# Running totals of a state space mixer made once for four token tiles, and broadcast by turning a column of step zero

## The reference, cut to what matters

```
a_cs = jnp.cumsum(ac, axis=-1)                       # within a tile of 128 tokens
seg = a_cs[..., :, None] - a_cs[..., None, :]
decay = jnp.exp(jnp.where(causal, seg, -jnp.inf))
...
decay_to_end = jnp.exp(a_cs[..., -1:] - a_cs)
chunk_decay = jnp.exp(a_cs[..., -1])
y_off = jnp.einsum('bclgn,bcgkpn,bcgkl->bclgkp', cm, prev, jnp.exp(a_cs))
```

## Time and profile before

| | |
|---|---|
| median of 3 runs | 2507.09 us (2497.56 to 2507.71) |
| time of the profiled execution | 2508.93 us |
| its span | 2506.9 us |
| mean granted TensorE clock | 0.966 |
| instructions | 29324 |
| DMA, mean over the span | 89 GB/s |

### The profile page before, as it was taken

One profiled execution on the slowest core, in us unless ns is written; L12 is line 12 of the kernel. 1 busy time (PEld: TensorE's weight loads), 2 busy tenths in 40 slices (PEclk: granted clock), 3 DMA queues, 4 the chain that ended last, 5 costly groups with the idle time before them and its releaser, 6 DMA issues.

```text
span 2506.9 us, 29324 instructions
## 1 busy us (share of the span) xinstructions
PE 2345.6 (94%) x11988; PEld 1945.1 (78%) x11988; DVE 1307.2 (52%) x1935; ACT 922.7 (37%) x1670; POOL 155.0 (6%) x115
## 2 busy tenths in 40 slices
PE   7997888898999999999898999999899899899988
PEld 6887676776888888888686788888697687788766
DVE  4997677654834334635463573334525526413444
ACT  3353563433423223344333333233334425323343
POOL 0000100040400000400021040000000000000000
PEclk9998989899999999999899999999899999999999
DMA  5322223432332323312332223333232121221102
GB/s 156 99 86 68 85 89 135 132 116 84 94 123 96 101 94 99 119 51 68 112 99 67 71 100 102 100 101 101 67 118 81 37 90 62 68 84 51 34 34 109
DMA packets 187195, 224.78 MB, mean 90 GB/s; under 512 B 16603, under 2 KB 153510, under 8 KB 186038
## 3 DMA queue, kind: packets, MB, share of 16 engines
q1 hardware_dynamic: 174800, 191.90, 24.3%
q10 hardware_dynamic: 11686, 22.62, 2.6%
q0 software_dynamic: 576, 8.39, 0.9%
HBM read 213.72 MB, written 9.18 MB: 89 GB/s over the span
## 4 chain that ended last, share of the span: by engine, by line
PE 82%; DVE 11%; ACT 5%; issue 2%; ACTq 1%; POOL 0%; DVEq 0%
PE gemm L588 24%; PE gemm L589 23%; PE gemm L590 23%; PE aux L720 2%; DVE y_plain L2284 2%; DVE w_lo L2078 2%; PE aux L972 1%; PE aux L953 1%; PE aux L1225 1%; DVE x_lo L2101 1%; DVE work L2216 1%; PE aux L1247 1%; ACT w_hi L1291 1%; PE aux L1238 1%; DVE w_lo L2074 1%
## 5 line engine op out<-in xcount | busy, mean ns | idle before, releaser
L588 PE MATMUL gemm<-x_hi,w_hi 128*128 128x512 f32 x1288 | 518.2, 402 | 10.3 <-DVE w_lo L2078 7.9
L2078 DVE TENSOR_TENSOR w_lo<-raw,w_hi 128x1024 fp32r<-128x1024 f32 x250 | 317.8, 1301 | 392.0 <-ACT w_hi L1291 391.3
L590 PE MATMUL gemm<-x_hi,w_lo 128*128 128x512 f32 x1288 | 505.9, 393 | 0.0
L589 PE MATMUL gemm<-x_lo,w_hi 128*128 128x512 f32 x1288 | 505.7, 393 | 0.0
L1291 ACT ACTIVATE w_hi<-raw 128x1024 fp32r<-128x1024 f32 x250 | 254.0, 1051 | 246.7 <-PE gemm L590 243.6
L588 PE MATMUL gemm<-w_hi,x_hi 128*128 128x256 f32 (+2 forms) x992 | 315.5, 318 | 10.3 <-DVE h L2165 5.4
L588 PEld LDWEIGHTS gemm<-x_hi,w_hi 128*128 128x128 f32 x1288 | 244.1, 190 | 87.8 <-issue 24.0
L589 PE MATMUL gemm<-w_lo,x_hi 128*128 128x256 f32 (+2 forms) x992 | 310.6, 313 | 0.0
L590 PE MATMUL gemm<-w_hi,x_lo 128*128 128x256 f32 (+2 forms) x992 | 310.2, 313 | 0.0
L590 PEld LDWEIGHTS gemm<-x_hi,w_lo 128*128 128x128 f32 x1288 | 244.0, 189 | 52.1
L589 PEld LDWEIGHTS gemm<-x_lo,w_hi 128*128 128x128 f32 x1288 | 244.5, 190 | 46.9
(11 more groups left out here) (328 smaller groups left out, 2880.7 us busy)
## 6 DMA issues: line engine op xcount, KB each, us to landing
raw<-in_mlp_w_dram SPq DMA_DIRECT2D x64, 1024.0 KB, 5.2
raw<-in_w_in_dram SPq DMA_DIRECT2D x31, 1024.0 KB, 5.3
raw<-in_odd_w_in_dram SPq DMA_DIRECT2D x12, 1024.0 KB, 5.3
raw<-in_even_w_in_dram SPq DMA_DIRECT2D x10, 1024.0 KB, 5.3
raw<-in_even_w_in_dram SPq DMA_DIRECT2D x16, 512.0 KB, 5.3
raw<-in_xa_w_k_dram SPq DMA_DIRECT2D x8, 1024.0 KB, 5.0
raw<-in_xa_w_v_dram SPq DMA_DIRECT2D x8, 1024.0 KB, 5.0
raw<-in_even_w_out_dram SPq DMA_DIRECT2D x8, 1024.0 KB, 5.2
```

Source lines behind the costliest of these rows:

```text
L588: pe.matmul(dst, a_hi, b_hi, start=first, stop=False)
L589: pe.matmul(dst, a_hi, b_lo, start=False, stop=False)
L590: return pe.matmul(dst, a_lo, b_hi, start=False, stop=last)
L2078: dve.tensor_tensor(w_lo[:, s % W_SLOTS, :, :], raw[:, s // 2 % RAW_SLOTS, :, half], w_hi[:, s % W_SLOTS, :, :].bitcast(F32), ALU.subtract)\
```

## The change

- The state space sums of all four tiles are made by one `running_sums()`, with a second product with all ones for the tiles' totals. VectorE's `tile_sums()` copies the sums over the steps in `sm[:, 0:4]`, the totals to `sm[:, 8:12]`, total less sum to `sm[:, 12:16]`, and releases ScalarE once, after that. It stands in pass n = 0; VectorE's `differences` and the later tile sums are gone.
- ScalarE's `sum_exps()` exponentiates these once, after the first `decays`; the two small Exps of each tile are gone.
- The rows of sums are no products any more. The sums are already in a column, and a transpose of the column read with step zero puts them in a row on all partitions: one `turn` a head in `sums_as_rows`, four a head in `key_sums`. Before the first of either, TensorE waits until VectorE has written the sums (`aux_read(pe, "acs")`, `aux_read(pe, "cc")`).

```diff
--- before.py
+++ after.py
@@ -140,12 +140,12 @@
     def tile(c):
         return [("bc", c, q) for q in range(4)] + [("cb", c), ("xs", c, 0), ("xs", c, 1), ("bt", c)]
 
-    e += [("acs", 0)] + tile(0)
+    e += [("acs",)] + tile(0)
     for c in range(TT):
         for g in range(2):
             e += [("yd", c, g)] + ([("yo", c, g)] if c else [])
         if c + 1 < TT:
-            e += [("st", c, g) for g in range(2)] + [("acs", c + 1)] + tile(c + 1)
+            e += [("st", c, g) for g in range(2)] + tile(c + 1)
         e += [("yt", c, g) for g in range(2)]
     e += [("ln", "conv", i) for i in range(2)]
 
@@ -281,7 +281,7 @@
         cst = sb("cst", [P, 4])
         mxs = sb("mxs", [P, 3, 4])
         rs = sb("rs", [P, 3, 4])
-        sm = sb("sm", [P, 16, SH])
+        sm = sb("sm", [P, 20, SH])
         stats = sb("stats", [P, TT, 2, 6])
         mean_var = sb("mean_var", [P, TT, 2])
         rstd = sb("rstd", [P, 2, TT])
@@ -812,10 +812,13 @@
             for t in range(TT):
                 ins = turn(dst[:, SH * t:SH * (t + 1)], DTR[:, t * P:(t + 1) * P])
             ins.then_inc(aux_done, 1)
-            def running_sums(c):
+            def running_sums():
 
                 pe.wait_ge(S["dta_ready"], 1)
-                pe.matmul(next_aux("acs", c)[:, 0:SH], triu[:, :], sm[:, c, :], start=True, stop=True)\
+                dst = next_aux("acs")
+                steps = sm[:, 0:TT, :].rearrange("p a b -> p (a b)")
+                pe.matmul(dst[:, 0:TT * SH], triu[:, :], steps, start=True, stop=True)
+                pe.matmul(dst[:, TT * SH:2 * TT * SH], ones[:, :], steps, start=True, stop=True)\
                   .then_inc(aux_done, 1)
 
             def sums_as_rows(c):
@@ -824,8 +827,7 @@
                     dst = next_aux("bc", c, q)
                     for j in range(4):
                         hd = 4 * q + j
-                        ins = pe.matmul(dst[:, j * P:(j + 1) * P], sm[:, c, hd:hd + 1].broadcast_to([P, P]),
-                                        triu[:, :], start=True, stop=True)
+                        ins = turn(dst[:, j * P:(j + 1) * P], sm[:, c, hd:hd + 1].broadcast_to([P, P]))
                     ins.then_inc(aux_done, 1)
 
             def memory_steps(count):
@@ -885,9 +887,10 @@
             turned_memory()
             gemm("conv_in", x_hi, x_lo, panels=2)
             gemm("xbc", x_hi, x_lo, panels=4)
-            running_sums(0)
+            running_sums()
             gemm("xbc", x_hi, x_lo, panels=2)
             gemm("z", x_hi, x_lo, panels=3)
+            aux_read(pe, "acs")
             tile_operands(0)
             gemm("z", x_hi, x_lo, panels=1)
             aux_read(pe, "mem", 3)
@@ -915,7 +918,6 @@
                     for g in range(2):
                         pe.matmul(next_aux("st", c, g)[:, :], BT[:, g, :], XW[:, 8 * g:8 * g + 8, :],
                                   start=True, stop=True).then_inc(aux_done, 1)
-                    running_sums(c + 1)
                     memory_steps(1)
                     tile_operands(c + 1)
                 else:
@@ -1243,15 +1245,14 @@
 
                 dst = next_aux("cb_c", hd)
                 for t in range(TT):
-                    for s in range(t + 1):
-                        ins = pe.matmul(dst[:, t * P:(t + 1) * P], sm[:, s, hd:hd + 1].broadcast_to([P, P]),
-                                        (triu if s == t else ones)[:, :], start=(s == 0), stop=(s == t))
+                    ins = turn(dst[:, t * P:(t + 1) * P], sm[:, 4 + t, hd:hd + 1].broadcast_to([P, P]))
                 ins.then_inc(aux_done, 1)
 
             def next_key_sums(u):
                 if u[1] == 1 and u[0] + 1 < 8:
                     key_sums(u[0] + 1)
 
+            aux_read(pe, "cc")
             key_sums(0)
             units("c", [(hd, t) for hd in range(8) for t in range(TT)], scores_c, turns_c, values_c, next_key_sums)
             turned_output("Ct", "c", 2)
@@ -1585,23 +1586,25 @@
 
             def differences(c):
 
-                r = 8 + 4 * (c % 2)
+                act.wait_ge(S["seg_ready"], 1)
                 for q in range(4):
-                    act.wait_ge(S["seg_ready"], 4 * c + q + 1)
                     bank = wait_aux(act, ("bc", c, q))
                     for j in range(4):
                         hd = 4 * q + j
                         ins = act.activation(M[:, hd, :], bank[:, j * P:(j + 1) * P], ACT.Relu, scale=-1.0,
-                                             bias=sm[:, r, hd:hd + 1])
+                                             bias=sm[:, c, hd:hd + 1])
                     free_aux(ins, ("bc", c, q))
 
             def decays(c):
 
-                r = 8 + 4 * (c % 2)
                 aux_read(act, "bc", c, 3)
                 act.activation(M, M, ACT.Exp, scale=-1.0).then_inc(S["decay_ready"], 1)
-                step(act.activation(sm[:, r + 1:r + 3, :], sm[:, r + 1:r + 3, :], ACT.Exp))
-                act.activation(sm[:, r + 3, :], sm[:, r, :], ACT.Exp).then_inc(S["dte_ready"], 1)
+
+            def sum_exps():
+
+                act.wait_ge(S["seg_ready"], 1)
+                act.activation(sm[:, 8:16, :], sm[:, 8:16, :], ACT.Exp)
+                step(act.activation(sm[:, 16:20, :], sm[:, 0:4, :], ACT.Exp))
 
             def tile_rows(c):
 
@@ -1636,10 +1639,10 @@
             gate_z(3)
             logs()
             decays(0)
+            sum_exps()
             conv_first(KC - 1)
             split_to(FIRST_PANEL["xk0"] + 1)
             for c in range(TT):
-                r = 8 + 4 * (c % 2)
                 if c:
                     if c == 3:
                         act.wait_ge(S["k_out"], 16)
@@ -1647,7 +1650,7 @@
                 if c + 1 < TT:
                     act.wait_ge(S["xdt_ready"], c + 1)
                     for hd in range(SH):
-                        ins = act.activation(XW[:, hd, :], XDT[:, hd, :], ACT.Copy, scale=sm[:, r + 1, hd:hd + 1])
+                        ins = act.activation(XW[:, hd, :], XDT[:, hd, :], ACT.Copy, scale=sm[:, 12 + c, hd:hd + 1])
                     ins.then_inc(S["xw_ready"], 1)
                 if c:
                     memory_rows(c - 1, 1)
@@ -2342,34 +2345,27 @@
                     dve.scalar_tensor_tensor(sm[:, 0:4, :], dt, -1.0, over(row16[:, 1, :], TT), ALU.mult, ALU.mult)\
                        .then_inc(S["dta_ready"], 1)
 
-            def tile_sums(c):
-
-                r = 8 + 4 * (c % 2)
-                bank = wait_aux(dve, ("acs", c))
-                free_aux(dve.tensor_copy(sm[:, r, :], bank[:, 0:SH]), ("acs", c))
-                aux_read(dve, "acs", c)
+            def tile_sums():
+
+                bank = wait_aux(dve, ("acs",))
+                rows = bank[:, 0:2 * TT * SH].rearrange("p (i t n) -> p i t n", i=2, n=SH)
+                step(dve.tensor_copy(sm[:, 0:4, :], rows[:, 0]))
+                dve.tensor_copy(sm[:, 8:12, :], rows[:, 1])
+                free_aux(dve.tensor_tensor(sm[:, 12:16, :], rows[:, 1], sm[:, 0:4, :], ALU.subtract), ("acs",))
+                aux_read(dve, "acs")
+                dve.engine_nop().then_inc(S["seg_ready"], 1)
 
             for n in range(4):
                 split_to(FIRST_PANEL["z"] + n + 1)
                 taps(6)
                 if n == 0:
-                    tile_sums(0)
+                    tile_sums()
                 if n == 1:
                     accumulate(0)
                 if n == 2:
                     accumulate(1)
             tri2 = over(triu[:, :], 2)
             cb = TMP[:, 0, 0:2 * P].rearrange("p (a b) -> p a b", b=P)
-
-            def differences(c):
-
-                r = 8 + 4 * (c % 2)
-                for q in range(4):
-                    bank = wait_aux(dve, ("bc", c, q))
-                    rows = bank[:, :].rearrange("p (a b) -> p a b", b=P)
-                    hs = slice(4 * q, 4 * q + 4)
-                    dve.tensor_tensor(sm[:, r + 1, hs], rows[:, :, P - 1], sm[:, r, hs], ALU.subtract)
-                    dve.tensor_copy(sm[:, r + 2, hs], rows[:, :, P - 1]).then_inc(S["seg_ready"], 1)
 
             xs = XS.rearrange("p (a b) -> p a b", b=SP_)
             skip = TMP.rearrange("p a b -> p (a b)").rearrange("p (a b) -> p a b", b=SP_)
@@ -2408,11 +2404,9 @@
                                                        ALU.mult, ALU.subtract)
                     free_aux(ins, ("yt", c, g))
 
-            differences(0)
             split_to(FIRST_PANEL["xk0"])
             tile_decays(0)
             for c in range(TT):
-                r = 8 + 4 * (c % 2)
                 if c:
                     turned_tile(c - 1)
                 dve.wait_ge(S["m_ready"], c + 1)
@@ -2435,7 +2429,7 @@
                         aux_read(dve, "yd", c, g)
                         free_aux(dve.tensor_tensor(skip[:, 8 * g:8 * g + 8, :],
                                                    bank[:, :].rearrange("p (a b) -> p a b", b=SP_),
```

(6 more changed lines are left out.)

## The result

The changed kernel takes 2474.61 us (median of 4 runs, 2472.49 to 2476.54), the kernel before 2507.05 us (2497.56 to 2507.71). The ratio is 0.9878, 95% interval 0.9859 to 0.9896. By the medians the change saves 32.4 us, 1.3%; by the ratio it is 1.2%. The size is firm to a few us only: three of the four runs before lie near 2507 and one at 2497.56, and by the means the change saves 30.3 us. The forecast was 2478 us, range 2465 to 2494. The profiled execution took 2472.49 us, its span is 2470.8 us.

A forecast was written before the change was run, and what follows sets the result against it. TensorE, busy 94% of the span, was taken as the bound. Gains 13.5 + 1.1 - 0.2 + 14.4 = 28.8 us put the profiled 2508.93 us at 2480.1, or 2478 us from the median; range 2465 to 2494.

The forecast's parts named there:

- Tile 0: State space part, tile 0: ScalarE released in pass n = 0, so z3 starts 13.5 us earlier.
- The smaller moves: State space tiles: dropped Exps gain 1.1 us, extra records in running_sums() lose 0.2, turns for rows give 0.
- Stage C: Rows of sums by four turns a head instead of 20 records: 1.5 us at head 0, 13.0 at the others, 14.4 together.
- The clock: Stage C: low-clock loss of 6.8 us kept unchanged in the sum; bounds 6.8 us gained and 28.4 us lost.
- Given back in the state space part: State space part: VectorE ends the section, the 13.5 us return as a wait for convolution taps; 2492 us, chance 0.07.
- Absorbed in stage C: Stage C: the wait before the transposes grows by what the rows lose, 14.4 us; 2493 us, chance 0.05.
- A turn at a product's price: Stage C: a turn is as dear as a product, taking 3.9 us off the gain; 2482 us, chance 0.04.
- A spell at each head: Stage C: a low-clock spell at each of 8 heads, 28.4 us lost; 2507 us, no change, chance 0.04.
- a stage mostly at the low clock: Stage C: the clock stays low through most of it, 96 us of low spells making 2520 us; chance 0.02.

The follow-up runs named there:

- e3: Changed kernel with VectorE's release of ScalarE moved behind the taps of pass n = 3: 2490.75 us, ratio 0.9928.
- e9: The changed kernel itself, unedited, measured again on another chip: 2471.49 us.
- e10: Changed kernel with the state space rows made by products again, early release kept, run beside e9: 2473.59 us.
- e11: Changed kernel with stage C's next row read earlier, room for all 16 tap diagonals, and ScalarE's Relus first at a tile's end: 2452.44 us, ratio 0.9795.
- e12: e11 with the rows of the state space part made by products: 2452.01 us.
- e1: Changed kernel with stage C's rows made by products again, the state space part keeping the change: 2487.69 us, ratio 0.9929.
- e2: Kernel before with only stage C's rows made by turns, behind the wait for the copy of the sums: 2489.31 us, ratio 0.9935.
- e5: Changed kernel with each turn of stage C's rows issued five times, 20 a head instead of 4: 2485.67 us.

## Why the prediction was right

- **Tile 0.** Put at 13.5 us. z3 came 14.4 - 0.8 = 13.6 us sooner, for the reason given: ScalarE's idle time before the Relus was 13.49 and is nothing, and e3 puts it back with the one moved release (z3 at 237.97 there). From the first Relu to z3 it took 4.6 us, as before. VectorE did not take the gain back; of its idle 17.01 us 5.22 are left, where I expected 3.5 and a little, as `differences(0)` and the wait for `cb` went too.
- **The smaller moves.** Put at 1.1 less 0.2. The part gained 14.9 in all, 1.3 beyond z3's 13.6. That is a sum of two things: behind z3 1.2 us are lost again, for the taps took 1.8 us longer with the clock's fall, and tiles 1 to 3 took 96.4 us instead of 98.9. Net, e3 against the kernel before gives 0.5. Whether the Exps gave their 1.1 the profiles can't resolve, and no run left only them out. The turns of the state space rows, put at 0, are 0 within 2 us by e9 and e10, e11 and e12.
- **Stage C.** Put at 14.4 us: 1.5 for head 0 (measured 4.73 - 3.34 = 1.4, from the start of the sums' product to the first scores, 2280.23 to 2284.96 before and 2261.39 to 2264.73 after), 1.85 for each other. The stage is 17.1 us shorter. By the clocks of the two stretches, 0.95 and 0.97, 0.05 / 0.5 x 136.75 / 2 = 6.8 us were lost before and 0.03 / 0.5 x 119.69 / 2 = 3.6 after; so 3.2 are the clock's and 13.9 the turns'. That is 12.5 for the seven other heads, where 13.0 were expected. The clocks have two figures only, so these parts are good to 1 us or so. The price of a turn, 0.11 us, held. The wait for VectorE's read stayed at 9.2 us, as the order of VectorE said it would.
- **The clock.** I left its loss as it was. This is the term of the sum that was off. It gave back 3 us in stage C and 3 in the unchanged stretch before it (added up over pieces of 4 us by their granted clocks, low clock cost that stretch 51.2 us before and 47.8 after); with 0.8 at the start this is the difference between the sum of 28.8 and the 36.1 of the spans. In the medians the difference is 3.7 us, and by the means the gain is 30.3, so it is partly luck how close the forecast came: runs of the kernel before alone lie 10 us apart. That stage C with the same code took 132.1 us in e1 and 136.75 in the kernel before says that what the clock gives back in the stage needn't be an effect of the turns. The waits of `cb`, forecast near 14 us, were 13.4.
- **The rivals.** Given back in the state space part: excluded by the 5.22 us of idle time and e1. Absorbed in stage C: excluded by e2. A turn at a product's price: excluded by 0.11 us a turn (four took 0.65 us and 20 took 2.35). A spell at each head, and a stage mostly at the low clock: the changed stage has two spells, not eight, and a mean of 0.97. By the Trainium skill's "TensorE: Matmul & The Clock Gate", Part 4, transposes don't count for the full clock. The trace of e5 disagrees for these float32 transposes: 0.99 over the stage with 20 turns a head, as with 20 product records in e1.

## What to carry to other kernels

Before an operation is made cheaper, ask what the engine waits for behind it: here 1.9 us a tile saved on the rows were worth nothing, and the same rows in stage C, with no wait behind them but one that moved with them, were worth all they cost. A release that stands behind other work in a hand-written order can be paid in full by whoever idles for it: 13.5 us for one release behind twelve taps here, and moving VectorE's read of one bank in stage C gave 12 us more. A profile's stretch in which nothing changed may still be 3 us shorter, and the same kernel measured 2474.61 us once and 2471.49 on another chip, so a kernel that seems better by such an amount has to run again side by side.

## What the runs showed of the hardware

- A float32 transpose of 128x128 with a column of step zero as its stationary operand costs 0.11 us in a run ((2.35 - 0.65) / 16, from 20 and four of them), like other transposes (1.75 us for 16 in the earlier trace rows), and like one of the two records of a float32 product of that size (3.73 us for 32 in the earlier trace rows).
- The granted clock held over float32 transposes as over products: 0.99 over stage C with 20 a head (e5) as with 20 product records (e1). At the stage's start it fell in every profile with four turns a head (0.91 over the first 20 us), and in none with 20 turns or 20 product records (1.00).
- Whether the clock falls behind a given pause can differ between two executions of one kernel: behind GpSimd's pause in the taps it did in one profile of the changed kernel (1173 ns for the longest record) and not in another (697 ns). Runs of the kernel before on one chip went from 2498.54 us at a granted clock of 0.971 to 2507.97 at 0.967.
